# Two of four modulation chunks moved from TensorE's columns to VectorE's products, in the mLSTM stage of a two-layer diffusion block on one Trainium2 core

## What is computed

```
silu_c = jax.nn.silu(c)
silu_cc = jax.nn.silu(c_ctx)
for l in range(DEPTH):
    mod = jnp.split((silu_c @ ada_w[l] + ada_b[l])[:, None, :], 6, axis=-1)
    mod_c = jnp.split(silu_cc @ ada_w[l] + ada_b[l], 6, axis=-1)
    ...
    x = x + mod[2] * rms_norm(y, mix_post_g[l])
    h = modulate(rms_norm(x, ffn_pre_g[l]), mod[3], mod[4])
```

## Time and profile before

| | us |
|---|---|
| three runs | 1673.02, 1669.77, 1673.84 (median 1673.02) |
| the profiled execution | 1669.0 |
| its span in the trace | 1667.3 |
| TensorE busy | 1607.5 (96% of the span) |
| VectorE busy | 1024.0 (61%) |
| ScalarE busy | 551.7 (33%) |
| mean granted TensorE clock | 0.989 |

### The profile page before, as it was taken

How to read it: one execution, slowest core, us unless ns; L and a number is a source line. 1 busy time by engine, 2 the same in 40 slices (tenths; PEclk the granted TensorE clock), 3 DMA queues, 4 the chain that set the end, 5 groups by cost and what they waited for, 6 DMA issues and landing times.

```text
span 1667.3 us, 21933 instructions
## 1 busy us (share of the span) xinstructions
PE 1607.5 (96%) x8698; PEld 1347.4 (81%) x8698; DVE 1024.0 (61%) x1457; ACT 551.7 (33%) x878; POOL 54.6 (3%) x74
## 2 busy tenths in 40 slices
PE   5999999999999999999999999898999999999998
PEld 2688887787898878888888887787778988888886
DVE  2899996659757774667626446654875644454344
ACT  3313224555633221123211225613325532232133
POOL 0500000210000000000000001100000000000001
PEclk9999999989999999999999999999999999999999
DMA  9421212334116552454323231230002233223222
GB/s 309 137 67 51 77 51 70 115 111 111 39 53 226 205 172 79 139 193 166 129 83 133 51 101 51 80 101 26 26 1 63 89 101 112 79 89 113 88 95 81
DMA packets 134009, 169.43 MB, mean 102 GB/s; under 512 B 15970, under 2 KB 92450, under 8 KB 133930
## 3 DMA queue, kind: packets, MB, share of 16 engines
q1 hardware_dynamic: 133360, 168.11, 31.5%
q10 hardware_dynamic: 570, 0.22, 0.1%
HBM read 166.17 MB, written 2.15 MB: 101 GB/s over the span
## 4 chain that ended last, share of the span: by engine, by line
PE 77%; DVE 14%; ACT 3%; issue 2%; POOL 1%; POOLq 0%; DVEq 0%; ACTq 0%
PE acc L700 39%; PE acc L755 21%; DVE conv_u L1845 7%; PE acc L726 4%; PE acc L912 2%; DVE w_lo L1570 2%; PE acc L1120 2%; PE acc L1099 2%; PE acc L813 1%; PE acc L947 1%; PE acc L1067 1%; PE acc L668 1%; DVE x L1745 1%; PE acc L925 1%; POOL y L2263 1%
## 5 line engine op out<-in xcount | busy, mean ns | idle before, releaser
L700 PE MATMUL acc<-h_hi,w_hi 128*128 128x512 f32 (+1 forms) x1424 | 414.1, 352 | 3.0 <-issue 2.4
L700 PE MATMUL acc<-h_lo,w_hi 128*128 128x512 f32 (+1 forms) x1424 | 411.1, 350 | 0.0
L700 PE MATMUL acc<-h_hi,w_lo 128*128 128x512 f32 (+1 forms) x1424 | 411.1, 350 | 0.0
L1570 DVE TENSOR_TENSOR w_lo<-raw,w_hi 128x1024 fp32r<-128x1024 f32 x183 | 219.6, 1229 | 155.6 <-ACT w_hi L1139 155.5
L700 PEld LDWEIGHTS acc<-h_hi,w_hi 128*128 128x128 f32 x1424 | 229.8, 188 | 40.6 <-issue 3.4
L1139 ACT ACTIVATE w_hi<-raw 128x1024 fp32r<-128x1024 f32 x183 | 186.5, 1055 | 225.8 <-PE acc L755 183.9
L700 PEld LDWEIGHTS acc<-h_lo,w_hi 128*128 128x128 f32 x1424 | 229.6, 188 | 37.4 <-issue 0.5
L700 PEld LDWEIGHTS acc<-h_hi,w_lo 128*128 128x128 f32 x1424 | 229.4, 188 | 37.2
L755 PE MATMUL acc<-w_hi,hid_hi 128*128 128x512 f32 x440 | 176.3, 401 | 0.0
L755 PE MATMUL acc<-w_lo,hid_hi 128*128 128x512 f32 x440 | 175.6, 399 | 0.0
L755 PE MATMUL acc<-w_hi,hid_lo 128*128 128x512 f32 x440 | 175.5, 399 | 0.0
(11 more groups left out here) (245 smaller groups left out, 2051.7 us busy)
## 6 DMA issues: line engine op xcount, KB each, us to landing
ada_w<-in_ada_w SPq DMA_DIRECT2D x88, 512.0 KB, 5.9
raw<-in_ffn_w_in SPq DMA_DIRECT2D x88, 512.0 KB, 3.6
raw<-in_ffn_w_out SPq DMA_DIRECT2D x44, 512.0 KB, 4.2
raw<-in_even_w_in SPq DMA_DIRECT2D x24, 512.0 KB, 4.5
ada<-in_ada_w SPq DMA_DIRECT2D x8, 1024.0 KB, 12.2
raw<-in_odd_w_in SPq DMA_DIRECT2D x12, 512.0 KB, 4.2
raw<-in_even_w_out SPq DMA_DIRECT2D x8, 512.0 KB, 4.5
ada_m<-in_ada_w SPq DMA_DIRECT2D x8, 512.0 KB, 4.4
```

What stands on the lines that cost most here:

```text
L700: last = nc.tensor.matmul(acc[:, s, m, t0:t1], w[:, slot, kk, c], x_[:, k, t0:t1], start=(k == 0 and q == 0), stop=(k == KD - 1 and q == 2))
L1570: return nc.vector.tensor_tensor(out_, in0, in1, op)
```

## The change

Chunks 0 and 1 are no longer multiplied by TensorE. VectorE multiplies the rows of the chunk by the conditioning value of their row (a scalar per partition) and adds up the eight row blocks, one sum for each of the two vectors (`ada_piece`). A chunk is 16 instructions of 128x256, cut into four pieces of four. Then TensorE only sums over the partitions: four instructions of one column against a column of ones (`ada_columns_m`). The pieces stand in VectorE's program right after `weighted` of the items in `ADA_PIECES`, the sums in TensorE's after (1, 3) and (2, 1). A half of `ada_m` is now free for the next chunk when VectorE has done its second piece (`adam_summed`). Chunks 2 and 3 stay as they were. The products use two areas of 2 KB inside the buffer of later modulation loads (`ada_w`), so that load waits for `adam_cols` too.

```
-ADA_PARTS = {(0, 4): (0, 1), (0, 5): (2, 3)}
-ADA_PARTS |= {(h, 2): (0, 1, 2, 3) for h in (1, 2, 3)}
+ADA_PARTS = {(h, 2): (0, 1, 2, 3) for h in (2, 3)}
+ADA_PIECES = {(0, 3): (0, 0), (0, 4): (0, 1), (0, 5): (0, 2), (1, 1): (0, 3),
+              (1, 2): (1, 0), (1, 3): (1, 1), (1, 4): (1, 2), (1, 5): (1, 3)}
+ADA_COLS = {(1, 3): 0, (2, 1): 1}
...
+        adam_s = [place(f"adam_s{e}", [P, 2, 256], offset=ADA + 14336 * e) for e in range(2)]
...
                     for half in range(2):
-                        if e:
-                            sp.wait_ge(adam_used, 2 * (e - 1) + half + 1)
+                        if e == 3:
+                            sp.wait_ge(adam_used, half + 1)
+                        elif e:
+                            sp.wait_ge(adam_summed, 2 * (e - 1) + half + 1)
...
             sp.wait_ge(sem("conv_normed"), 4)
+            sp.wait_ge(adam_cols, 2)
             load_beside("out0", w_even_out, 0, (("c", 0),))
-            sp.wait_ge(adam_used, 8)
+            sp.wait_ge(adam_used, 4)
...
+            def ada_columns_m(e):
+
+                pe.wait_ge(adam_summed, 2 * e + 2)
+                for x_ in range(2):
+                    for s in range(2):
+                        c = 944 + 4 * e + 2 * x_ + s
+                        last = nc.tensor.matmul(acc[:, 0, 1, c:c + 1], adam_s[e][:, s, x_ * P:(x_ + 1) * P], ones[:, 0:1],
+                                                start=False, stop=True, skip_group_check=True)
+                last.then_inc(adam_cols, 1)
...
                     for part in ADA_PARTS.get((hd, q), ()):
                         ada_part(hd, part)
+                    if (hd, q) in ADA_COLS:
+                        ada_columns_m(ADA_COLS[hd, q])
...
                 if hd == HEADS - 1:
-                    dve.wait_ge(adam_used, 8)
+                    dve.wait_ge(adam_used, 4)
+                    dve.wait_ge(adam_cols, 2)
...
+            def ada_piece(e, q):
+
+                half = q // 2
+                if q % 2 == 0:
+                    dve.wait_ge(adam_full[half], 16 * (e + 1))
+                for kk in (2 * (q % 2), 2 * (q % 2) + 1):
+                    for s in range(2):
+                        w, scale = ada_m[:, half, kk, :], cond[:, 4 * half + kk, s:s + 1]
+                        if half == 0 and kk == 0:
+                            ins = nc.vector.tensor_scalar(adam_s[e][:, s, :], w, scale, None, ALU.mult)
+                        else:
+                            if not half or kk:
+                                sd.wait(sd.value() - 1)
+                            elif not s:
+                                dve.wait_ge(adam_summed, 2 * e + 1)
+                            ins = nc.vector.scalar_tensor_tensor(adam_s[e][:, s, :], w, scale, adam_s[e][:, s, :], ALU.mult, ALU.add)
+                        if kk == 3 and s == 1:
+                            ins.then_inc(adam_summed, 1)
+                        else:
+                            sd.done(ins)
...
+                if (hd, q) in ADA_PIECES:
+                    ada_piece(*ADA_PIECES[hd, q])
                 if q == 0 and hd:
                     reverse_sums(hd - 1)
```

More of the change, by code:

```diff
@@ L339, in build @@
         adam_full = [sem("adam_full0"), sem("adam_full1")]
-        adam_used = sem("adam_used")
+        adam_used, adam_summed, adam_cols = sem("adam_used"), sem("adam_summed"), sem("adam_cols")
         h_ready, h0_ready = sem("h_ready"), sem("h0_ready")
```

## The result

| | before | after |
|---|---|---|
| runs of the same comparison, median | 1671.39 us (6 runs, 1669.52 to 1673.84) | 1679.49 us (6 runs, 1672.63 to 1681.90) |
| ratio | | 1.0043, 95% interval 1.0027 to 1.0059 |
| the profiled execution, its span | 1669.0, 1667.3 us | 1681.9, 1680.2 us |
| TensorE's mean granted clock | 0.989 | 0.986 |

A forecast was written before the change was run, and what follows sets the result against it. VectorE was taken as the bound from (1, 3) to `forward_sums` of head 1, with TensorE waiting for it. Terms 1.1 + 4.9 + 0.2 = +6.2 us on 1673.0 gave 1679.2 us, range 1674.0 to 1684.5.

The forecast's parts named there:

- The price of a piece: On VectorE, four 128x256 instructions at 0.41 us each: 1.64 us, bounds 1.10 to 1.91; a chunk's first piece 1.42 us.
- Head 0: End of head 0: three pieces, 4.70 us, go before `forward_sums`, 3.30 us of it into idle time; +1.4 us.
- Up to (1, 2): Head 1: `head_inverse` hidden, chunk 1 on TensorE filled a wait, removing it gives 0.3 us; shift now +1.1 us.
- (1, 3) to (1, 5): Head 1: three pieces of 1.64 us in VectorE's stretch without idle time, all on the path; +4.9 us.
- The clock: Head 1: TensorE's 4.6 us at the lower clock from 324 us left as is; full clock taken for items behind.
- I take the full clock: (1, 3) to (1, 5): TensorE, though less busy after the change, was assumed to keep its full clock.
- the first rival: Clock also falls in (1, 3) to (2, 0): `weigh` of (2, 0) doubles, +2.5 us, in all +8.7; chance 0.14.
- Head 2: Chunk 1's sums after `weigh` of (2, 0): 0.84 us against 0.67 us idle ahead of `weigh` of (2, 2); +0.2 us.
- Loads: SP's queue waits for VectorE's pieces, but chunk 2's last half and the row maxima copies arrive in time; nothing.
- Faster: VectorE takes all eight pieces in idle time, TensorE gains 6.2 us: 1666.8 us; decided at (1, 3); chance 0.06.

The follow-up runs named there:

- half_pieces: The changed kernel with two instructions instead of four in each chunk 1 piece at (1, 3), (1, 4), (1, 5); ratio 1.0035 to the kernel before.
- chunk0_vector: The kernel before with only chunk 0 on VectorE, at the change's places and with its own buffer; ratio 1.0015.
- chunk0_out: The kernel before without chunk 0's load, TensorE parts or pieces; four one-column sums of a constant in its place; ratio 0.9985.
- chunk1_out: The kernel before without chunk 1's load, TensorE parts or pieces; four one-column sums of a constant in its place; ratio 1.0009.
- before_again: The kernel before, unchanged, profiled a second time; 1669.99 us.
- sums_added: The kernel before with four one-column TensorE instructions on a constant added after `weigh` of (2, 0), nothing on VectorE moved; ratio 1.0013.
- idle_head1: The kernel before with chunk 0's 16 instructions on VectorE, all in head 1 where VectorE had idle time; ratio 0.9993.

## Why the prediction was right

- **The price of a piece**, 0.41 us: 4.97 us for the three pieces of (1, 3) to (1, 5) against 4.9, and 0.39 to 0.43 us each in half_pieces. The first piece of a chunk, 1.26 us from neighbour to neighbour, is 0.16 under its 1.42. The place between the 128- and the 512-element rows was well chosen.
- **Head 0**, +1.4: measured +1.0. The three pieces take 1.26 + 1.53 + 1.58 = 4.37 us in VectorE's queue, not 4.70; less 3.30 of idle time that is 1.07. chunk0_vector and chunk0_out show both sides of the exchange: +1.0 with the pieces, -3.1 with neither.
- **Up to (1, 2)**, +1.1: measured +0.8 to +1.0. chunk1_out shows that chunk 1 covered a wait, as argued. `head_inverse` stayed hidden: `weigh` of (1, 2) still began behind GpSimd's mask and `weighted`, after the same 1.51 us.
- **(1, 3) to (1, 5)**, +4.9: measured +4.97, and nearly linear. This is the main term, and it is on the path in full.
- **The clock.** The prediction read the kernel before wrongly here: it counted 4.6 us at the lower level in head 1, from a window that begins at 324 us, but by windows of 2 us the clock was down from about 322 us, during chunk 1, for 6.8 us, and in before_again for 3.4. The change did not leave it alone either. In the first profile it cost head 1 less (+0.2 instead of +1.1 at `weighted` of (1, 3)), in the second it cost the same as before and the shift was +6.0, the forecast's figure to that place. "I take the full clock", said of (1, 3) to (1, 5), did not hold, so the first rival happened in part: the clock fell at the end of these items in one profile, at no cost up to `forward_sums`, and right behind them in the other, at 1.55 us in `weigh` of (2, 0). Its sum, +8.7 us, did not come: in the first profile the clock was up again before (2, 0), and in the second it stayed up later in head 2. The Trainium skill ("TensorE: Matmul & The Clock Gate", the section on the HAM clock gate) says that only sustained activity releases the full rate; the window from 340 us (0.59), behind one in which TensorE was busy for 2.39 of 4 us, agrees with it, and the trace of before could not show it.
- **Head 2**, +0.2: this term was mis-sized. It priced the sums by their length beyond the slack and took head 2's clock, and with it chunk 2 and what follows, to be as before. Head 2 lost 1.8 us in the change and 1.7 in sums_added, where (1, 3) to (1, 5) are not thinned, so the loss comes with the sums: 0.2 for their length and some 1.5 for the clock, low for 6.8 us instead of 3.4. No rival has this; the first has a loss of 2.5 us at `weigh` of (2, 0), another place and another cause. That the stage's +6.1 comes so close to +6.2 is luck: the 1.6 us too little in head 2 were made good by 0.8 us less in head 1 and 0.9 less in head 3, where the clock was low, around (1, 2) and in head 3, for 3.4 us less than in the first profile of before. Against before_again it is +6.7 to +6.9.
- **The time.** The 1679.49 us measured against 1679.2 forecast are luck as well: the forecast stands on a median before of 1673.0 us in three runs, which is 1671.39 in six. The difference is the fair measure, +7.2 against +6.2.
- **Loads** cost nothing: no wait on the path was put down to one. **Faster** failed at the point named for it: VectorE had no idle time at (1, 3) to (1, 5).

Of the change itself there are two profiles, one with head 2's loss and one without, so how often it is there is not known. What decides between 3.4 and 6.8 us at the lower clock in a head is open as well: sums_added shows that four short instructions are enough to go along with it, not why.

## What to carry to other kernels

Before work is moved off a busy engine, look at which wait ends last where it stood and at the exact stretch of the other engine's queue where it will stand: 4.46 us on the chain were worth 0.1 us at most, and three pieces of 1.64 us on an engine that is idle 39% of the time cost 4.97, all of their length. Sixteen such products, of the other chunk, put into that engine's waits made the stage 0.6 us longer than none at all (idle_head1 against chunk0_out), which is within what two profiles of one kernel differ by. A term below a microsecond on a TensorE whose clock goes up and down should carry a bound of a microsecond or two for the clock: 0.84 us of added work, of which 0.67 had slack, cost 1.7.

## What was not expected of the hardware

- VectorE's work beside GpSimd's masks seems to delay them. In idle_head1 and in chunk0_out the first mask of (1, 2) began 10.9 us after `forward_sums`, but that mask took 0.62 us instead of 0.29, and `weighted` followed 0.73 us behind its start (321.64, 322.37) instead of 0.40 (320.76, 321.16); VectorE was ready for it in both. `weigh` of (1, 2) was 0.35 us later. Nothing was run for this alone.
- TensorE's lower clock in the attention stage was 6.8 us in some profiles and up to 17.1 in others, and the time behind the output stage's start was 2.6 to 4.9 us longer in the latter, about as much as what was measured here. By size the clock can have made this, since 10.3 us more at half rate make at most 5.2, but it was not varied by itself, so how much of it is the clock's is not shown.
